# First steps of four stages done inside the stage before them, and no semaphore clearing ahead of the routing

## What is computed

```python
u = layernorm(x) * (1 + sc1) + sh1
qm, km, vm, om, gates, cq, ckv, kr = split(u @ w_in)
q, k = silu(conv5(qm, km))                 # 4 heads of 128
for each 128-token chunk, in two directions:      # matrix memory (mLSTM)
    w = exp(d_log - m); s = (q k^T) * w; a = exp(inter - m)
    num = a * (q C) + s v; den = a * (q n) + sum(s)
    h = num / max(|den|, exp(-m));  C = decay * C + (k * wg)^T v
h_m = sigmoid(om) * headnorm(h_fw + h_bw)
cq, ckv = rmsnorm(cq), rmsnorm(ckv)        # latents: 384 and 256 wide
q_nope, q_rope = cq @ w_uq; k_nope, v_a = ckv @ w_ukv    # rotary on q_rope, kr
o_a = softmax((q_nope k_nope^T + q_rope k_rope^T) * scale) v_a   # 4 heads
y = concat(h_m, rmsnorm(o_a)) @ w_out
x = layernorm(2**0.25 * x + (1 + g1) * y) * ln1_g + ln1_b
```

## Time and profile before

| what | value |
|---|---|
| median of 3 runs | 1534.84 us (1532.27 to 1535.22) |
| profiled execution | 1532.22 us |
| its span | 1530.4 us |
| mean granted TensorE clock | 0.989 of full speed |
| TensorE, matmul busy | 1481.8 us (97%) |
| VectorE busy | 564.9 us (37%) |
| ScalarE busy | 361.2 us (24%) |

### The profile page before, as it was taken

How to read it: one execution, slowest core, us unless ns; L and a number is a source line. 1 busy time by engine, 2 the same in 40 slices (tenths; PEclk the granted TensorE clock), 3 DMA queues, 4 the chain that set the end, 5 groups by cost and what they waited for, 6 DMA issues and landing times. The chain is left out here.

```text
span 1530.4 us, 19870 instructions
## 1 busy us (share of the span) xinstructions
PE 1481.8 (97%) x7339; PEld 812.6 (53%) x7340; DVE 564.9 (37%) x1134; ACT 361.2 (24%) x746; POOL 97.5 (6%) x97
## 2 busy tenths in 40 slices
PE   7999999999989999999999899999999999999997
PEld 4555554448768566665555544444444444444443
DVE  2222126567869333335767711111111011011118
ACT  1122122138734344443111010110111111111111
POOL 0000002000000000000000011111111111111110
PEclk9999999999999999999999899999999999999999
DMA  9401011128830200004111589869789779999975
GB/s 342 160 28 42 0 7 30 43 61 249 267 102 1 110 0 0 0 0 163 69 55 55 209 337 390 364 250 418 311 331 422 313 314 418 423 382 402 424 282 207
DMA packets 101797, 305.49 MB, mean 200 GB/s; under 512 B 18353, under 2 KB 61661, under 8 KB 92536
## 3 DMA queue, kind: packets, MB, share of 16 engines
q1 hardware_dynamic: 93064, 287.08, 48.9%
q0 software_dynamic: 8064, 16.80, 3.0%
q10 hardware_dynamic: 624, 1.03, 0.2%
HBM read 289.86 MB, written 25.76 MB: 206 GB/s over the span
## 5 line engine op out<-in xcount | busy, mean ns | idle before, releaser
L1926 PE MATMUL ps<-w_down_sb,hidT 128*128 x320 | 153.4, 612 | 0.0
L457 PE MATMUL ps<-w_in_tok,uT 128*128 128x512 f32 (+2 forms) x384 | 141.5, 529 | 0.0
L1910 PE MATMUL ps<-w_gate_sb,x_slotsT 128*128 x320 | 140.7, 592 | 0.7 <-ACT x_slotsT L2009 0.7
L1910 PE MATMUL ps<-w_up_sb,x_slotsT 128*128 x320 | 140.6, 592 | 0.0
L1581 PE MATMUL ps<-uT,hT 128*128 128x512 f32 x256 | 112.8, 594 | 0.0
L624 PE MATMUL ps<-uT,mod 128*128 128x512 f32 x256 | 111.0, 593 | 0.8 <-PEq L213 0.8
L2163 DVE TENSOR_TENSOR hid<-silu_g,ps 128x512 f32<-128x512 f32 x20 | 13.8, 688 | 258.4 <-PE ps L1910 258.4
L457 PEld LDWEIGHTS ps<-w_in_tok,uT 128*128 128x128 f32 x384 | 72.6, 190 | 65.5 <-issue 43.9
L1910 PEld LDWEIGHTS ps<-w_gate_sb,x_slotsT 128*128 128x128 f32 x320 | 60.7, 190 | 76.9 <-issue 76.9
L1910 PEld LDWEIGHTS ps<-w_up_sb,x_slotsT 128*128 128x128 f32 x320 | 60.8, 190 | 76.5 <-issue 76.5
L1926 PEld LDWEIGHTS ps<-w_down_sb,hidT 128*128 128x128 f32 x320 | 55.8, 189 | 65.1 <-issue 64.3
(11 more groups left out here) (407 smaller groups left out, 1916.4 us busy)
## 6 DMA issues: line engine op xcount, KB each, us to landing
light_gate_sb<-in_w_gate SPq DMA_DIRECT2D x20, 2048.0 KB, 11.5
light_up_sb<-in_w_up SPq DMA_DIRECT2D x20, 2048.0 KB, 16.2
light_down_sb<-in_w_down SPq DMA_DIRECT2D x20, 2048.0 KB
w_gate_sb<-in_w_gate SPq DMA_DIRECT2D x12, 2048.0 KB
w_up_sb<-in_w_up SPq DMA_DIRECT2D x12, 2048.0 KB, 17.6
w_down_sb<-in_w_down SPq DMA_DIRECT2D x12, 2048.0 KB
mod<-in_w_ada SPq DMA_DIRECT2D x8, 1024.0 KB, 8.2
w_ada_late<-in_w_ada SPq DMA_DIRECT2D x8, 1024.0 KB, 6.4
```

The costliest lines, as they stand in the source:

```text
L457: mm = nc.tensor.matmul(ps[:, 2 + g, 0:n], self.uT[:, k, t * P:(t + 1) * P], wt[:, k, c0:c0 + n], start=k == 0, stop=k == KD - 1)
L1910: m = m_.matmul(ps[:, bank, :], xT[:, k, :], wt[:, bass.ds(buf, 1), k, :].rearrange("p a f -> p (a f)"), start=k == 0, stop=k == KD - 1)
L1926: m = m_.matmul(ps[:, 5 + half, :], hT[:, k, :], wd[:, bass.ds(buf, 1), k, half * 512:half * 512 + 512].rearrange("p a f -> p (a f)"), sta ...
```

## The change

1. Matrix memory, first step. The `ab` of both directions and the W of direction 0, with both masks, move into `project_channels`; W and ab get a buffer of their own (the maxima rows use the same buffer before). The state is cleared by GpSimd. The transpose of the second direction's keys moves from before the first outer products to behind them. The filler at the end of the stage is gone.
2. Latents, first step. Tile 0 is scaled, transposed and scaled into latT inside the last halves of `mlstm`; its semaphores are kept through the clearing. `latent_projections` begins with the products of tile 0. Values are made in `products1`. The rotated q has two buffers. No filler.
3. Attention, first step. `latent_projections` ends with products1(6), turn(7), products1(7), the first pair of scores, products2(6), products2(7); the copies of q, the maxima and the first two exponentials move there. The loop makes the exponentials of the next pair at the end of each step; the last step is written out.
4. Output projection, first step. Square, root and gain of attention tile 0 are done at the end of `attend`, and attn_g is loaded there. No filler between the turns of tile 0.
5. Routing. No clearing; the waits for the stores of u2 and x1 go to GpSimd, VectorE and SP inside `experts`.

```diff
-                self.clear_semaphores(kept=[*self.s_gg, self.s_wkv])
+                self.clear_semaphores(kept=[*self.s_gg, self.s_wkv, *self.s_lat])
...
-            self.clear_semaphores()
@@ project_channels, ScalarE
+                for d in range(2):
+                    act.wait_ge(self.s_mb[d][0], 16)
+                    for h in range(H):
+                        op = a.activation(self.ml_ab[:, d, h, :], self.mb0[:, d, h, :], ACT.Exp, bias=self.mext[:, d, d * (TT - 1) + 1, h:h + 1], scale=-1.0)
+                    op.then_inc(self.s_ml["a"][d], 1)
                 act.wait_ge(s_lmm, 2)
                 a.copy(raw[:, 1, T // 2 + 2:T + 2], ps[:, 3, :]).then_inc(s_lraw, 1)
+                act.wait_ge(self.s_ml["mm"][0], 1)
+                for h in range(H):
+                    op = a.activation(self.ml_w[:, 0, h, :], self.ml_w[:, 0, h, :], ACT.Exp, bias=self.acol[:, 0, 0, h:h + 1], scale=-1.0)
+                op.then_inc(self.s_ml["w"][0], 1)
@@ project_channels, VectorE, convolved_last
+                        if n == 1:
+                            masked(0)
+                            masked(1)
@@ mlstm, ScalarE
-                decays(0, 0)
+                decays(0, 1)
                 keys(0, 0)
-                decays(0, 1)
                 keys(0, 1)
                 decays(1, 0)
                 kept(0, 0)
...
+                    if k == len(HALVES) - 4:
+                        a.copy(tn[:, QL + KVL:].rearrange("p (a b c) -> p a b c", a=1, b=2), self.kr2[:, 0:1]).then_inc(s_kr, 1)
+                for j in range(2):
+                    act.wait_ge(self.s_gg[j], 16)
+                act.wait_ge(s_tr, 1)
+                for l in range(NL):
+                    op = a.mul(self.latT0[:, l, :], ps[:, l // 4, (l % 4) * P:(l % 4 + 1) * P], self.lat_g[:, l:l + 1])
+                op.then_inc(s_cT, 1)
@@ mlstm, TensorE
+                def first_latent_turn():
+                    for j in range(2):
+                        pe.wait_ge(s_keep[j], TT // 2)
+                    pe.wait_ge(s_n, 1)
+                    pe.wait_ge(s_kr, 1)
+                    for j in range(NL + 1):
+                        m = t.transpose(ps[:, j // 4, (j % 4) * P:(j % 4 + 1) * P], tn[:, j * P:(j + 1) * P], self.c(C_ID))
+                    m.then_inc(s_tr, 1)
...
-                key_turns(0, 1)
                 pe.wait_ge(s_c0, 1)
                 for k, (i, d) in enumerate(HALVES):
                     outer(i, d)
+                    if k == len(HALVES) - 1:
+                        first_latent_turn()
                     if k > 0:
                         partial(k)
+                    else:
+                        key_turns(0, 1)
                     memory(i, d)
...
-                self.keep_clocked(2, 3)
@@ mlstm, VectorE
-                masked(0, 0)
-                masked(0, 1)
-                v.memset(cst8[:], 0.0).then_inc(s_c0, 1)
...
+                    if k == len(HALVES) - 2:
+                        ch.link(v.tensor_tensor(tn[:, 0:QL].unsqueeze(1), self.cq[:, 0:1, :], self.rlat[:, 0, 0:1].unsqueeze(2).to_broadcast([P, 1, QL]), ALU.mult))
+                        v.tensor_tensor(tn[:, QL:QL + KVL].unsqueeze(1), self.ckv[:, 0:1, :], self.rlat[:, 1, 0:1].unsqueeze(2).to_broadcast([P, 1, KVL]),
+                                        ALU.mult).then_inc(s_n, 1)
                     rows(i, d)
@@ latent_projections, VectorE
-                norm(0)
+                norm(1)
                 centred(0)
                 variance(0)
                 for t in range(TT):
-                    if t + 1 < TT:
+                    if t > 0 and t + 1 < TT:
                         norm(t + 1)
...
+                dve.wait_ge(self.s_S, 1)
+                self.maximum(ch, 0)
+                self.maximum(ch, 1)
@@ latent_projections, ScalarE
+                a.copy(self.krT[:, 0:P], ps[:, NL // 4, (NL % 4) * P:(NL % 4 + 1) * P]).then_inc(s_tre, 1)
+                key_tile(1)
                 squared(0)
-                turned(0, 0)
                 std(0)
...
+                    if t == 0:
+                        act.wait_ge(s_qne, 2)
+                        act.wait_ge(s_qrte, 2)
+                        a.copy(self.qs[:], self.qnT[:, 0])
+                        a.copy(self.qrs[:], self.qrT[:, 0]).then_inc(self.s_q, 1)
+                values(TT - 1)
+                self.exponent(act, 0, 0)
+                self.exponent(act, 1, 1)
+                queries(TT - 2)
+                queries(TT - 1)
@@ latent_projections, TensorE
-                turn(0)
-                self.keep_clocked(7, 2)
-                for t in range(TT):
+                for t in range(TT - 2):
                     products1(t, t % 2)
-                    if t + 1 < TT:
-                        turn(t + 1)
+                    turn(t + 1)
                     products2(t, t % 2)
-                self.keep_clocked(7, 1)
+                products1(TT - 2, 0)
+                turn(TT - 1)
+                products1(TT - 1, 1)
...
+                pe.wait_ge(self.s_q, 1)
+                self.pair_scores(0)
+                products2(TT - 2, 0)
+                products2(TT - 1, 1)
@@ attend
-                pe.wait_ge(s_q, 1)
-                scores(0)
-                self.keep_clocked(6, 2)
...
-                with act.Fori(0, TT) as t:
+                def step(t, last):
                     for g in range(2):
                         n = t * H + 2 * g
-                        exponent(n, 0)
-                        exponent(n + 1, 1)
                         turned(n, 0)
...
                         turned(n + 1, 1)
+                        if not last or g == 0:
+                            self.exponent(act, n + 2, 0)
+                            self.exponent(act, n + 3, 1)
+
+                with act.Fori(0, TT - 1) as t:
+                    step(t, False)
+                step(TT - 1, True)
+                a.activation(self.sqh[:], self.oa[:, 0, :], ACT.Square, accum_out=self.ro[:, 0:1]).then_inc(self.s_osq, 1)
+                act.wait_ge(self.s_oms, 1)
+                a.activation(self.ro[:, 0:1], self.ro[:, 0:1], ACT.Sqrt).then_inc(self.s_ostd, 1)
...
+                dve.wait_ge(self.s_ag, 16)
+                v.scalar_tensor_tensor(out=self.oa[:, 0, :], in0=self.oa[:, 0, :], scalar=self.ro[:, 0:1], in1=self.ag[:],
+                                       op0=ALU.mult, op1=ALU.mult).then_inc(self.s_oan, 1)
@@ output_projection
-                            if t == 0:
-                                self.keep_clocked(7, 4)
...
-                for j in range(2):
-                    sp.wait_ge(s_st[j], 16 * TT // 2)
-                sp.wait_ge(s_x1st, 16 * TT)
@@ experts: SP, GpSimd, VectorE ahead of the one-hots
+                sp.wait_ge(self.s_x1st, 16 * TT)
...
+                for j in range(2):
+                    pool.wait_ge(self.s_u2st[j], 16 * TT // 2)
...
+                for j in range(2):
+                    dve.wait_ge(self.s_u2st[j], 16 * TT // 2)
```

More of the change, by code:

```diff
@@ L1372, in _ @@
                         pe.wait_ge(s_p, n + 2)
-                        scores(1 - g)
+                        self.pair_scores(1 - g)
                         pe.wait_ge(s_td, t * 2 + g + 1)
```

217 lines of the change are left out of this document (122 added, 95 removed).

## The result

| what | before | after |
|---|---|---|
| median (of 4 runs each) | 1533.55 us (1531.88 to 1535.22) | 1518.88 us (1516.36 to 1519.21) |
| ratio | | 0.9908, 95% interval 0.9892 to 0.9925 |
| profiled execution, its span | 1532.22, 1530.4 us | 1519.21, 1517.3 us |
| mean granted TensorE clock | 0.989 | 0.991 |
| TensorE matmul busy | 1481.8 us | 1466.9 us |

What follows compares the result with a forecast made beforehand. The prediction took TensorE to bound the stages between handovers, with VectorE nearly full in the latent tiles. Its terms, 0.4 - 1.05 - 1.4 - 2.5 + 0.3 - 2.45 - 1.1 = -7.8, took 1534.84 to 1527.0 us; range 1523 to 1532.

Steps and rivals of the forecast that it cites:

- Start of the matrix memory: First step of the matrix memory: a late second `kw` on ScalarE makes the path 0.4 us longer.
- Rival C: Matrix memory: ScalarE's delay passes into every half and costs 3.5 us; total -4.3, 1530.5 us; chance 0.06.
- Drain: End of the matrix memory: filler before the clearing goes, ScalarE's copy and scalings come last; 1.05 us saved.
- First latent tile: First latent tile: VectorE decides, with one norm and part of the square root's wait gone; 1.4 us more saved.
- rival A: Two handovers: without filler TensorE's clock falls, costing 1.7 us each; total -4.4, 1530.4 us; chance 0.16.
- Last tile to attention: Last latent tile up to the attention loop: reordered products bring the loop's first scores earlier; 2.5 us saved.
- Attention loop: Inside the attention loop: the table load falls there once more, delaying TensorE by about 0.24; 0.3 us longer.
- all seven hidden: Lower bound for the attention loop: all seven exposed table loads become hidden; 1.7 us saved.
- Attention to output: Last attention tile to first output product: square already done, gain row already landed; 2.45 us saved.
- Output to routing: Logits to routing: without the clearing 1.38 us becomes 0.3; 1.1 us saved, bounds -0.5 and -3.1.
- rival B: Ahead of the routing: TensorE's clock stays up, the ranking comes 2.0 us earlier; total -9.8, 1525.0 us; chance 0.12.

Runs made afterwards that it cites:

- b_exp_first: The kernel before with one exponential of a 128x1 tile put on ScalarE just ahead of the attention loop; ratio 0.9971 to the kernel before.
- a_sqrt_first: The changed kernel with one square root of a 128x1 tile put on ScalarE just ahead of the attention loop; ratio 0.9917 to the kernel before.
- b_no_clearing: The kernel before with no clearing ahead of the routing and the waits for the stores moved into the experts; ratio 0.9989 to the kernel before.
- a_clearing: The changed kernel with only the clearing ahead of the routing put back; ratio 0.9927 to the kernel before.
- a_q6_early: The changed kernel with tile 6's q products put between the last latent turn and tile 7's products on TensorE; ratio 0.9923 to the kernel before.

## Why the prediction was wrong, step by step

- *Start of the matrix memory, +0.4.* Measured 11.64 in place of 11.06 from the start to the scores at the fallen clock, +0.6; at full clock it is 10.0, -1.0. The late second `kw` and the wait of 3.2 behind it came as said. That the sign hangs on the clock was not seen. Rival C, that the delay passes into every half, did not come: from VectorE's seventh add of the late modulation to its twelfth it is 25.04 before and 25.03 after.
- *Drain, -1.05.* The two together, -0.65, are +0.09 in the profiled pair, but the stage scatters: 96.57 is the mean of five profiles with the old stage (96.23 to 97.16), 95.36 of five with the new one: -1.2, which stands for -0.5 to +0.3 where the clock fell at the start and about -2.8 where it did not, in the mix that these profiles happened to have. VectorE's first latent operation was 0.35 earlier, 0.7 was forecast. The six transposes took 0.74 (431.63 to 432.37) where the forecast had 0.65; its 0.11 a record is 0.12 by its own row, 1.95 over 16.
- *First latent tile, -1.4.* -1.47, and TensorE idled 1.85 for the rotation, 2.4 forecast. Right, for the reason given: VectorE decides; the wait for the root was 0.56, 0.65 forecast. That is also why rival A's fall there cost nothing. The argument against it, a stretch at full clock in one profile, was weak: two of the five profiles in the old order fall at this tile too, all nine with the change do, and from VectorE's first operation to the loop it is 83.53 or 83.54 in the five, fallen or not, and 79.67 to 79.69 in the seven of the nine whose order in this stage is the changed kernel's.
- *Last tile to attention, -2.5.* -2.37; 1.49 of waiting for the scalings, 1.65 forecast. Right.
- *Attention loop, +0.3.* **This step failed.** It was -3.83. "The table load now falls inside the loop once more" took the load as part of the loop's code, where it depended on the table set at the loop's entry, which part 3 changes; b_exp_first shows that this alone is worth 3.73. It also took the load to cost in the new order what it cost in the old; a_sqrt_first shows seven loads there at no cost, so with the loads still in place the term would have been about -3.8 too. And "its old exposed seven times, and each delays TensorE by about 0.24" priced it by one wait. In a pass with the load TensorE's weight loads waited twice for the probabilities, 0.24 at the turn (608.44) and 0.24 at the scores (609.54), and the first part of the scores took 0.10 longer behind the stop: 3.63 from 609.54 to 613.17, 3.53 from 598.28 to 601.81. The price was to be had from the trace of before by the distance of the scores in a half with the load and without it: 609.54 - 598.28 = 11.26 against 620.46 - 609.54 = 10.92, and the second still carries that 0.10; without loads both are 10.82, so a pass lost 0.54. Even the bound of "all seven hidden", -1.7, was less than half of it. The Trainium skill (ScalarE: Activation LUTs, What ACT_TABLE_LOAD costs) has a drain on top of the 1.28, 2.66 in all; the trace disagrees. The load at 605.89 ends at 607.17, the first exponential starts at 607.18, and from the copy's start to the exponential's it is 2.32 with the load (604.86 to 607.18) and 0.90 without it in b_exp_first (603.09 to 603.99): 1.42 for the load.
- *Attention to output, -2.45.* -2.56. Right, with a gap of 2.1 on TensorE where 2.3 was forecast. The clock fell there in four of nine profiles; the profiled execution was one of the five.
- *Output to routing, -1.1.* -1.07 to VectorE's first operation, right. The further -2.0 was its lower bound and rival B, at a chance of 0.12; against the other three profiles with the clearing it is -0.5 to -0.7. "The fall came before the filler began, after transposes and narrow products that stay" was the wrong argument: those stayed, and the clock did too. b_no_clearing and a_clearing show that the gap decides it, 1.6 against 0.5 us, but for the one of ten that fell with 0.5.

The terms that held come to 8.7 with the stage means (1.2 + 1.47 + 2.37 + 2.56 + 1.07), where 8.1 was forecast. The loop's 3.8 and the 2.0 that the clock gave at the routing make it 14.5, of which a fall behind attention takes 0.8 to 2.3 back where it comes. With the 0.6 that the clock gave against the other profiles it is 13.1; the ratio's 14 (12 to 17) does not tell the two apart.

The forecast of 1527.0 missed the median by 8.1: 4.1 of that is the loop's step, 0.5 to 2.0 the routing's clock, and 1.3 the median of before, which stood at 1534.84 when the forecast was made and at 1533.55 with the fourth run. The rest is within the spread of the runs. With the loop's measured -3.8 in place of +0.3 the forecast would have been 1522.9, below the range's end of 1523.

## What to carry to other kernels

Price a stall that recurs in a loop by the length of the iterations with it and without it, not by the one wait that the profile names. Before a hardware loop, look which activation table its entry carries: one small activation of the right kind can take the loads out of every pass. An order that puts the load where the engine waits anyway does as well. A handover on TensorE is worth its gap and, from about 1.6 us of it on in these traces, also a clock that may or may not fall behind it. A fall costs only where TensorE sets the pace: nothing at the first latent tile, up to 2.3 us behind attention. Filler in the gap kept the clock in the two profiles that had it; that it lowers the time is not shown. And one profile of before and one of after do not price a stage whose clock differs between executions.

## What the runs showed of the hardware

The gap on TensorE at each handover, and in how many of the fourteen profiles its clock fell to 1.2 GHz in it or within 2 us behind it. The last four lines are waits inside a stage:

| handover | gap, us | fell |
|---|---|---|
| start of the matrix memory, old order | 1.97 to 1.98 | 1 of 5 |
| the same, changed kernel | 1.90 to 1.91 | 5 of 7 |
| the same with one more filler call | 1.04 | 0 of 2 |
| first latent tile, old order | 2.81 | 2 of 5 |
| the same, changed kernel | 2.42 to 2.51 | 9 of 9 |
| attention loop, a_q6_early | 2.97 | 1 of 1 |
| attention loop, all others | 0.84 to 1.22 | 0 of 13 |
| output products, part 4 without filler | 2.10 to 2.11 | 4 of 9 |
| the same, old order or with filler | 0.38 to 1.07 | 0 of 5 |
| routing, with the clearing | 1.59 to 1.61 | 4 of 4 |
| routing, without it | 0.53 | 1 of 10 |
| matrix memory, scores of the second step | 2.69 to 3.23 | 9 of 12 |
| the same place, kept copy early | 1.58, 1.93 | 0 of 1, 1 of 1 |
| first latent tile, second wait | 1.60 to 1.90 | 0 of 9 |
| last latent tile, five scalings | 1.49 | 0 of 8 |

So in these traces no gap of up to 1.5 us brought the clock down (the one case at the routing had fallen 1.5 us before the logits copy), and the longer ones did so in some executions and not in others. Length alone does not order them: 1.6 us ahead of the routing fell each time, 1.6 to 1.9 us inside the first latent tile never, 2.0 us ahead of the matrix memory once in five. Behind the same gap of 1.6 us the fall took between 8.63 and 10.09 us of filler. The loads of the table set, 1.28 us each, came and went in the loop with one instruction outside it. And the matrix memory, with the same instructions, took from 93.5 to 96.9 us in five profiles, in two groups by the clock at its start: 1.6 us of the distance stand at the scores of the second step (10.0 against 11.6), and the rest comes later, in waits and falls that differ between the profiles.
